# Hybrid mLSTM and sparse-attention decoder step: the input projection as three rounded products, with the weight chunk as outer loop

## What is computed

```python
def project(x, g_mix_l, w_in_l):
    p = rmsnorm(x, g_mix_l) @ w_in_l      # (.., 1024) @ (1024, 3664)
    ...                                   # split: mq mk mv mo mi mf aq ak av iq ik iw
def mlstm_mixer(...):
    qk, new_buf = causal_conv(concatenate([mq, mk]), conv_buf, conv_w_l); qk = silu(qk)
    ig = mi + bg[:4]; lf = log_sigmoid(mf + bg[4:])
    h, C, n, m = mlstm_chunkwise(q, k, v, ig, lf, C0, n0, m0)
def attn_inputs(...):
    q = rope(rmsnorm(aq, g_q), pos); k = rope(rmsnorm(ak, g_k), pos); qi = rope(iq, pos); ki = rope(ik, pos)
def select_keys(qi, w, ki, qpos, key_pos, topk):
    scores = einsum('bth,bths->bts', w * 8 ** -0.5, relu(einsum('bthd,bsd->bths', qi, ki) * 64 ** -0.5))
    _, idx = top_k(where(visible, scores, -inf), topk)      # 128 keys of a prompt row, 256 of a sample row
```

## Time and profile before

| | us |
|---|---|
| median of three runs | 2339.48 |
| lowest and highest of them | 2325.98, 2359.36 |
| span of the profiled execution | 2321.8 |
| lowest run less that span | 4.2 |
| PE busy, share of the span | 2143.2, 92% |
| DVE busy | 1047.4, 45% |
| ACT busy | 410.6, 18% |
| POOL busy | 67.8, 3% |
| mean granted TensorE clock | 0.899 |

### The profile page before, as it was taken

The page is one execution under the profiler, slowest core; times in us unless marked ns, Lnnn a source line. Parts: engine busy times, 40 slices in busy tenths (PEclk is TensorE's granted clock), DMA queues, the critical chain, the costliest instruction groups (busy, mean ns, idle before and its releaser), DMA issues. The chain is left out here.

```text
span 2321.8 us, 29058 instructions
## 1 busy us (share of the span) xinstructions
PE 2143.2 (92%) x11170; PEld 1595.7 (69%) x11170; DVE 1047.4 (45%) x2048; ACT 410.6 (18%) x870; POOL 67.8 (3%) x92
## 2 busy tenths in 40 slices
PE   6989978889998999999988899788999989999998
PEld 5434357566457999999953434655664679999998
DVE  2217685568203433345412195945770043333453
ACT  1022112242301000031011221123332010000400
POOL 0000011200000000000000000121000000000000
PEclk8989987755999999999979899867559989999999
DMA  3111131041412223223132112111414012322231
GB/s 115 69 37 52 49 94 39 22 131 48 132 37 73 73 73 99 84 65 86 51 98 72 37 25 95 39 39 50 137 50 132 24 50 73 110 73 91 58 101 64
DMA packets 193701, 165.26 MB, mean 71 GB/s; under 512 B 30882, under 2 KB 173506, under 8 KB 193554
## 3 DMA queue, kind: packets, MB, share of 16 engines
q1 hardware_dynamic: 193554, 163.32, 22.8%
HBM read 153.57 MB, written 9.71 MB: 70 GB/s over the span
## 5 line engine op out<-in xcount | busy, mean ns | idle before, releaser
L884 PE MATMUL psum<-ring,xn 128*128 128x512 f32 (+1 forms) x800 | 354.5, 601 | 0.0
L884 PEld LDWEIGHTS psum<-ring,xn 128*128 128x128 f32 (+1 forms) x800 | 138.6, 176 | 197.7 <-issue 197.2
L901 PE MATMUL psum<-xn,ring 128*128 128x272 f32 x1024 | 243.8, 399 | 30.0 <-ACT rawr L746 26.7
L936 PE MATMUL psum<-x_high,w_split_even 128*128 128x272 f32 x1408 | 247.3, 294 | 16.1 <-DVE x_low L1688 16.1
L901 PEld LDWEIGHTS psum<-xn,ring 128*128 128x128 f32 x1024 | 197.5, 194 | 74.3 <-issue 29.1
L936 PE MATMUL psum<-x_high,w_split_odd 128*128 128x272 f32 x1408 | 237.6, 288 | 0.0
L936 PEld LDWEIGHTS psum<-x_high,w_split_even 128*128 128x128 f32 x1408 | 205.4, 193 | 20.6 <-issue 20.6
L917 PE MATMUL psum<-h_high,w_split_even 128*128 128x272 f32 x1232 | 204.4, 287 | 1.7 <-issue 1.7
L936 PEld LDWEIGHTS psum<-x_high,w_split_odd 128*128 128x128 f32 x1408 | 199.5, 188 | 0.0
L1712 DVE TENSOR_TENSOR proj<-rawr,psum 128x544 f32<-128x544 f32 x44 | 31.7, 721 | 333.9 <-PE psum L936 333.9
L917 PEld LDWEIGHTS psum<-h_high,w_split_even 128*128 128x128 f32 x1232 | 173.3, 188 | 2.5 <-issue 2.5
(11 more groups left out here) (344 smaller groups left out, 2568.0 us busy)
## 6 DMA issues: line engine op xcount, KB each, us to landing
ring<-in_w_gate_up_dram SPq DMA_DIRECT2D x44, 1024.0 KB, 7.1
ring<-in_w_in_dram SPq DMA_DIRECT2D x14, 2048.0 KB, 7.8
ring<-in_w_down_dram SPq DMA_DIRECT2D x16, 1408.0 KB, 6.9
ring<-in_w_out_dram SPq DMA_DIRECT2D x4, 2048.0 KB, 8.0
ring<-in_cache_k_dram SPq DMA_DIRECT2D x48, 128.0 KB, 2.0
cq<-in_cache_k_dram SPq DMA_DIRECT2D x48, 128.0 KB, 2.0
R<-in_cache_kidx_dram SPq DMA_DIRECT2D x128, 32.0 KB, 1.7
qk<-in_state_C_dram SPq DMA_DIRECT2D x16, 256.0 KB, 3.9
```

What stands on the lines that cost most here:

```text
L884: mm = pe.matmul(out[0:r, 512 * (t % 2):512 * (t % 2) + 512], xnv[:, k, c:c + r], w[:, k, :], start=(k == 0), stop=(k == KT - 1))
L901: mm = pe.matmul(out[:, 512 * hf:512 * hf + HALF], w[:, k, c:c + P], src[:, k, HALF * hf:HALF * hf + HALF], start=(k == 0), stop=(k == nk ...
L936: mm = pe.matmul(out[:, 512 * hf:512 * hf + HALF], w_part(f, w)[:, k, u, :], v[:, k, HALF * hf:HALF * hf + HALF], start=(k == 0 and q == 0 ...
```

## The change

The input projection goes to three rounded products as well. With xh, xl the two parts of the normed activations and high, low those of the weights:

```diff
-PICKS_CONV, PICKS_PROMPT = 7, 21
+PICKS_CONV, PICKS_PROMPT = 0, 24
-CONV0 = 1 + 5 * 3
+CONV0 = 1 + 5 * 5
 # PE
+                def token_chunk(s, k, tiles=range(5)):
+                    high, low = chunk_high(s, k), slab_low(1 + s)[:, k, :]
+                    pe.wait_ge(s_w_low, chunk_unit(s, k) + 1)
+                    for t in tiles:
...
+                        for q, (v, w) in enumerate(((xh, high), (xl, high), (xh, low))):
+                            mm = pe.matmul(ps(t)[0:r, :], v[:, k, c:c + r], w, start=(k == 0 and q == 0), stop=(k == KT - 1 and q == 2))
...
+                def conv_tile(m):
...
+                        for q, (w, v) in enumerate(((high, xh), (high, xl), (low, xh))):
+                            for hf in range(2):
+                                mm = pe.matmul(out[:, 512 * hf:512 * hf + HALF], w[:, k, :], v[:, k, HALF * hf:HALF * hf + HALF],
```

```diff
+                def cast_chunk(s, k):
+                    if k == 0:
+                        slab_arrived(pool, 1 + s)
...
+                    if k >= 4:
+                        pool.wait_ge(s_w_used, 7 * s + k - 3)
...
+                    pool.tensor_copy(chunk_high(s, k), slab_view(1 + s)[:, k, :]).then_inc(s_w_high, 1)
+                def low(unit, whole, high, out):
+                    pool.wait_ge(s_w_high, unit + 1)
+                    pool.tensor_tensor(out, whole, high.bitcast(F32), ALU.subtract).then_inc(s_w_low, 1)
```

The work between the slabs is now put between chunks. On PE: gate rows turned behind chunk (0, 1), gate columns behind (1, 3), index queries between (2, 0) and (2, 3), four index dots ahead of each of the chunks (3, 0) to (3, 5), and each sample sequence's index keys in two halves around the tiles of one chunk:

```diff
+                fill = ([(3, 6)], [(3, 7)], [(4, 0), (4, 1)], [(4, 2)], [(4, 3)], [(4, 4), (4, 5)], [(4, 6)], [(4, 7)])
+                for b in range(DB):
+                    turn_index_keys(b, 0)
+                    if b >= 1:
+                        index_dots(b - 1, 0)
+                    token_chunk(*fill[b][0], range(0, 3))
+                    turn_index_keys(b, 1)
...
+                conv_tile(0)
+                index_dots(7, 0)
+                index_dots(7, 1)
...
+                mm.then_inc(s_snew, 1)
+                conv_tile(1)
```

ACT does the gate rows ahead of its copies of slab 0 (IQ), and its reciprocal roots for the attention queries and keys stay behind the copies of slab 4 and the relu of the new index keys (`s_snew`). On DVE the gate rows come ahead of the rope of the index queries, and the picks of the prompt move:

```diff
 # DVE, behind the 24 accumulations
-                for j in (1, 2, 3):
-                    dve.wait_ge(s_masked, j)
-                    pick(penv[:, j - 1, 0:(j + 1) * P], P, TOPK_P)
-                dve.wait_ge(s_out_free, 10)
+                dve.wait_ge(s_out_free, 1 + 5 * 3)
 ...
                 rope(qk, 8, 4, rawr).then_inc(s_qk_ready, 1)
+                for j in (1, 2):
+                    dve.wait_ge(s_masked, j)
+                    for _ in range(TOPK_P // 8):
+                        pick_round(j)
+                    picked(j)
+                dve.wait_ge(s_masked, 3)
 ...
 # DVE, mLSTM loop, each of the sixteen steps
+                    pick_round(3)
```

More of the change, by code:

```diff
@@ L60 @@
 DOWN0 = FFN0 + 2 * FT
-SLOTS = {"small": 1, "tok": 3, "conv": 4, "out": 4, "ffn": 4, "down": 1}
+SLOTS = {"small": 1, "tok": 5, "conv": 4, "out": 4, "ffn": 4, "down": 1}
+CHUNK0 = 1
+FEAT0 = CHUNK0 + 5 * KT
 def slots_before(i):
@@ L306, in build @@
         penv = pen[:, :].rearrange("p (j s) -> p j s", j=3)
-        gr = cq[0:MH, 0:7 * T].rearrange("p (r t) -> p r t", r=7)
+        gr = ([rawr[0:MH, T * r:T * r + T] for r in range(3)]
+              + [proj[0:MH, 8720 + T * r:8720 + T * r + T] for r in range(4)])
         rm, ra = pen[0:MH, 0:T], pen[0:MH, T:2 * T]
@@ new lines, in _ @@
+                low(0, slab_view(0), small_high, slab_low(0))
+                for s in range(3):
+                    for k in range(KT):
+                        low_chunk(s, k)
+                for k in range(KT):
+                    low_chunk(3, k)
+                    if k in (3, 5, 7):
+                        j = k // 2 - 1
+                        pool.wait_ge(s_relu_free, IH * (j + 1))
+                        blk = penv[:, j, (j + 1) * P:(j + 2) * P]
+                        pool.affine_select(out=blk, in_=blk, compare_op=ALU.is_ge, fill=NEG, base=0,
+                                           pattern=[[-1, P]], channel_multiplier=1).then_inc(s_masked, 1)
@@ L555, in _ @@
+                pool.wait_ge(s_gate_cols_turned, 1)
                 pool.memset(mv[:, 0:4, :, P:P + 1], 1.0)
                 pool.memset(mv[0:NS, 4, :, P:P + 1], 1.0).then_inc(s_ones_set, 1)
[L557 to L562, removed]
@@ L661, in _ @@
                 norm(s_sq1, s_sum1, s_rstd1, rstd)
+                for k in range(KT):
+                    act.wait_ge(s_xn_scaled, k + 1)
+                    act.activation(xh[:, k, :], sqv[:, k, :], ACT.Copy).then_inc(s_xn_high, 1)
                 src = slot(0)[:, 0:400].rearrange("p (t c) -> p t c", t=5)
@@ L1059, in _ @@
+                mm.then_inc(s_sscore, 1)
+                for m in range(2, 8):
+                    conv_tile(m)
                 pe.wait_ge(s_out_free, OUT0)
@@ L1389, in rope @@
                     return ins
-                dve.wait_ge(s_out_free, 4)
+                dve.wait_ge(s_gate_turned, 1)
+                dve.wait_ge(s_gate_in, 16 * 7)
+                for q in range(2):
+                    dve.tensor_scalar(gr[q][:, 0:SEQ], ps(5 + q)[0:MH, :], bgate[:, q:q + 1], None, ALU.add)
+                    ins = dve.tensor_scalar(gr[q][:, SEQ:T], ps(7)[0:MH, NS * q:NS * q + NS], bgate[:, q:q + 1], None, ALU.add)
+                ins.then_inc(s_gate_read, 1)
+                dve.wait_ge(s_gate_read, 1)
@@ new lines, in _, with seqs @@
+                dve.wait_ge(s_gate_log, 1)
+                step(dve.scalar_tensor_tensor(out=gr[1], in0=gr[1], scalar=0.0, in1=gr[2],
+                                              op0=ALU.min, op1=ALU.subtract))
+                step(dve.tensor_tensor_scan(gr[2], rm, gr[1], 0.0, ALU.mult, ALU.add))
+                step(dve.tensor_tensor(gr[0], gr[0], gr[2], ALU.subtract))
+                step(dve.tensor_copy(gr[1], gr[0]))
+                def seqs(row):
+                    return row[:, SEQ:T].rearrange("p (b t) -> p b t", b=DB)
```

479 lines of the change are left out of this document (265 added, 214 removed).

## The result

The changed kernel takes 2382.84 us (median of four runs, 2378.99 to 2385.18), the kernel before beside it 2348.62 (four runs): a ratio of 1.0166, 95% interval 1.0107 to 1.0226. It is slower, by 1.1 to 2.3%, and 2% counts as a difference here. Ratios leave out executions more than 1.5% above the fastest of their kernel, which ran at a lower granted clock; of e9_before_reordered these are two of four (2320.24 and 2323.94 us at 0.89, against 2285.12 at 0.91 and 2306.92 at 0.90; 2313.58 is the median of all four), and its trace is of one of them.

What follows compares the result with a forecast made beforehand. Each layer was taken as a chain: PE up to the roots, DVE from there to the last convolution, then the mLSTM loop. Terms of -21.6 + 4 + 22 + 11 + 2.5 = +17.9 us a layer, +36 in all, gave 2375 us, range 2325 to 2430.

Steps and rivals of the forecast that it cites:

- The likeliest case: Whole kernel: the summed terms hold, 2375 us, own range 2345 to 2405; chance 0.55.
- Q: The point where ACT's reciprocal roots come, 295.2 us before; forecast at about 273.6 in the first layer.
- the two waits of PE over 20 us: Conv stage, a sign to look for: PE waits over 20 us for the third conv tile and again for the sixth.
- Term 6: From the rope's end to the last convolution: picks of blocks 1 and 2 land here; +22 us a layer.
- Rival C: Conv stage: picks aren't on the path, PE sets the pace; -18 instead of +22 a layer, 2295 us; chance 0.08.
- Term 1: Norm and small slab: more subtractions, last k later; +11 us a layer (+4 to +14).
- Term 2: From the small slab to the end of the index dots, thirty chunks; -10.3 us a layer.
- Terms 3 and 4: The eight key steps, -30.6 us a layer, then the rest up to Q, +8.3.
- Term 7: mLSTM loop: sixteen pick rounds (24.3 us) added, partly taken up by DVE's waits; +11 us a layer (+6 to +16).
- Term 8: Attention: three more sample pick rounds on DVE; +2.5 us a layer.
- Rival A: Projection chunks: POOL becomes the bound, 4.0 us a chunk pair instead of 2.5; 2429 us; chance 0.17 with the slow matmul.
- Rival B: DVE beside POOL: the port costs two-input work nothing, 39 us go; 2336 us, no change; chance 0.20.

Runs made afterwards that it cites:

- e9_before_reordered: Kernel before, projection still float32: ACT's roots behind step u = 1, DVE's squares, scaling and rope ahead of its prompt picks; 2296 us, ratio 0.9819.
- e1_roots_early: Changed kernel with ACT's reciprocal roots moved behind its copies of slab 3, not behind the last relu; 2285.24 us, ratio 0.9724.
- e2_picks12_in_gap: Changed kernel with DVE's picks of blocks 1 and 2 moved ahead of its wait for the roots; 2330.75 us, ratio 0.9977.
- e7_roots_picks_spread: Changed kernel with e1_roots_early's roots, POOL's output-gate products behind its key scaling, and picks spread over DVE's gaps; 2249.18 us, ratio 0.9572.
- e4_pool_cast_twice: Changed kernel with every token chunk's cast made twice on POOL; 2385.14 us, ratio 1.0157.
- e5_pe_busy: Changed kernel with unused padding products on PE ahead of and within the small slab; 2375.68 us, ratio 1.0105.

## Why the prediction was right, and where its terms were not

The forecast was 2375, +36 on the median shown, in a range of 2325 to 2430; it came to +34 between the medians beside each other. The likeliest case, in which PE's saving ahead of Q goes to DVE's picks behind it, is what the stages show, down to the two waits of PE over 20 us that were named (25.2 and 22.2), and e1_roots_early and e2_picks12_in_gap bear it out by taking the picks off the path in two ways. That the number is so close is in part luck. The sum was worked out from the trace, and trace against trace it is +28.8 a layer and not +17.9, the span 2377.3 and not 2358: 19 us short. The medians hide that: the span before lies 27 us below the median beside it (2321.8, 2348.62), the span after 6 (2377.3, 2382.84).

- **Term 6, the heart of it: right.** +22.7 for +22, with picks of 36.4 us (308.7 to 345.2) and PE's saving on the conv tiles worth nothing, as written. Without the picks there, two things I didn't see come up: the convolutions get 9 us longer beside POOL (e1_roots_early, e2_picks12_in_gap), and behind them PE would bound the stage at some 354, 32 of the 36.5 us earlier. Rival C stood that close behind.
- **Term 1: the clock was left out.** I took 125 ns for an 80-column product, which holds at the full clock (110 measured). The slab ran at half clock, as its predecessor had at 0.51 after 43 us. The row that cut this stage should have been read for its clock, too. The parts as I wrote them (55, 12 and 1) also give 68 and not 66.6. In turn the port cost less than feared: POOL had its four chunks split by 44.4, and DVE's norm work was back at its lengths alone (0.77 and 0.71) from 44.9 on.
- **Term 2: the 5 us wait for bank 0 never came.** The gate chain took 16.4 us from the turned rows (80.9) to ACT's last exponential (97.3), not 23 to 28: I had charged ten for the port, and DVE's rows of the chain took 9.7 us (86.0 to 95.7) instead of 6.3. PE went from chunk to chunk meanwhile. The chunk itself was 3.47 us (231 ns a product, inside 215 to 250), not 3.33.
- **Terms 3 and 4: 5.5 us too good.** Ten chunks at 3.47 give 1.4 of it. PE's waits for index keys by DMA, 4.4 us a layer, are about the 4 I had put. The rest lies in the steps' turns and dots, and wasn't taken apart.
- **Term 7: +16.3 for +11,** at the upper end of its range. DVE's old waits of 18.5 us took up 8 of the 24.3, not 13. What the sum left out is again the clock: 0.65 over the loop and not 0.81, with PE busy for 50.1 us and not 39.7, and in e7_roots_picks_spread the same loop differs by 12.9 us between its layers at 0.85 and 0.63. No run splits the clock's share from that of the picks.
- **Term 8: +5.3 for +2.5,** for three more rounds of 2.6 us. DVE's waits hid less of them than I put; no run takes it apart.
- **Rival A** is refuted as a price by e4_pool_cast_twice and by POOL's waits for PE; beside DVE's rope a pair did take up to 4.06 us, and the lead took it up. **Rival B** holds in part: the gate chain and the norm paid less than charged, the convolutions paid 3 us a tile where they met a split, and 7 to 8 where they met the product of the output gate too.
- **POOL's cast.** It took 0.61 us for 512 columns. I had let the scaling of 544 columns (1.57) stand for it. The Trainium skill, "GPSIMD Engine Reference", section "Engine selection", puts one-input work at roughly line rate; the cast, at 1.2 ns a column, agrees with that better than the scaling of keys, also one input, which still takes 1.57 us (2.9 ns a column). Nothing in the sum hung on it, since PE's chunk is longer than either.

## What to carry to other kernels

Before an engine is made faster, find what stands in program order behind its last result: here ACT's roots, four small instructions, stood behind all of ACT's copies and held DVE idle for 69 us a layer. Count the work that the change moves behind that point, and give the moved work a gap of its own engine to sit in; a few blocks moved in three of the five functions turned 1.7% slower into 4% faster. And test the old kernel with the new order before the gain is credited to the new arithmetic: here half of the 4% was there without it.

## What the runs showed of the hardware

- DVE and POOL hold each other up in both directions. Six two-input instructions of 512 columns took 2.8 us alone, 5.8 beside a cast and a subtraction of 1024 columns (3.9 us of POOL), 5.0 beside the subtraction alone (2.4); POOL's subtraction of 512 columns took 1.3 alone and 2.4 beside DVE's rope. The Trainium skill, "SBUF — State Buffer", section "Who interferes with whom", makes the ports that DVE and POOL share an exclusive lock, held for the whole instruction. The delays of 3.0 us beside 3.9 of POOL and 2.2 beside 2.4 agree with that roughly, and the cast, which has one input, counts as well.
- In e5_pe_busy the granted clock fell from full to half at 58.5 us, with PE busy without a gap since 53.2 with 80-column products alone. In the changed kernel it was 0.50 throughout 52.5 to 71.1, where PE was busy with them for 17.9 of 18.6 us, and rose at 74.0, within chunk (0, 0). A PE that the profile shows busy is thus no proof of the full clock.
- The same instructions of the mLSTM loop took 46.8 us in one layer and 59.7 in the other of one execution, at granted clocks of 0.85 and 0.63 (e7_roots_picks_spread). A stage's clock has to be read before its length is put down to an edit.
